# The running sum over the convolution's channels: in one row behind the last tap, not between the taps

## The chip, the cores and the metric

The kernel runs on one core of a Trainium2 chip. The metric is the device time of one execution in microseconds (us). The core's engines run side by side and meet only at semaphores: PE (TensorE, matrix products), DVE (VectorE), ACT (ScalarE), POOL (GpSimd) and SP (SyncE, which starts transfers).

## The reference, cut to what matters

Two layers of a decoder trunk over 528 tokens (16 meta tokens and 512 of the sequence), width 1024, in float32:

```
u = rms_norm(h, norm_mix); proj = u @ w_in          # glu, q, k, v, gates
a = glu_a * sigmoid(glu_b)
a = causal_depthwise_conv(a, conv_w, conv_b)        # 31 taps per channel
a = silu(layer_norm(a, conv_ln_g, conv_ln_b))       # mean and variance over the 1024 channels
y_conv = a @ w_pw + b_pw
y_attn = rms_norm(diff_attention(q, k, v, lam), subln)
h = h + (sigmoid(g_conv) * y_conv + sigmoid(g_attn) * y_attn) @ w_o
h = h + square(relu(rms_norm(h, norm_mlp) @ w_up)) @ w_down
```

The layer norm needs, for every token, the sum of the convolution's output over all channels. That sum is what the change moves.

## The kernel before, in words

Channels lie on the 128 partitions in eight tiles, tokens along the free dimension. Each layer runs as GLU (convolution inputs), five attention stages (0 to 4), a last part with the gates, the layer norm and the pointwise product, the output projection, and the MLP. Weights stream in as slabs of 128x2048, split into a high and a low half so that PE can multiply in three passes: POOL makes both halves (`split`, L505 to L518), and in the attention stages only the low half, in 16 pieces of 128x128 (`split_low`, L520 to L525), after ACT has made the high one. POOL also makes the rotary products of q and k (`turn`, L569 and L570).

The convolution is DVE's. The first 11 taps of six tiles are made in the GLU part, the remaining 182 (list `LATE`, two tiles at a time) in the attention stages by the generator `late_taps`. A tap is one instruction over 128x512 that accumulates in PSUM (L461, L462); the last tap of a tile writes it to `conv` in SBUF. DVE's order in the stages is written out by hand in `VECTOR_ORDER`: a number is so many taps, the names stand for the attention's steps (`m` maxima, `c` combination, `sub` mean square, `q`/`k` evictions, `rq`/`rk` rotation, `g` an early gate's eviction), and `ln`, in stage 4, stands for the rest of the taps and `ln_sums`. PE's order is in `MATRIX_ORDER`. Both engines work strictly in these orders.

The running sum is kept in `r_inv2[:, META:T]`. Behind the last tap of tile 1 tiles 0 and 1 are added (L473), behind those of tiles 3 and 5 two tiles each (L476), all inside `late_taps`; `ln_sums` adds tile 6 (L1397) and announces it with the semaphore `ln_ready`. PE sums that tile and tile 7 over the partitions with a product by ones (`channel_sums`, L674). Ahead of it stand these two waits on PE, of which the second is for the eviction of the last early gate:

```python
pe.wait_ge(exp_done, (layer + 1) * HEADS * 2 * 3)
pe.wait_ge(a_free[1], (layer * A_TILES + A_GATE + EARLY_GATES) // 2)
channel_sums(layer, ln_ready, layer + 1, [r_inv2[:], conv[:, NT - 1, :]], st_full)
```

On DVE that eviction (L1292, the `g` behind `ln`) follows `ln_sums`. PE's last work in stage 4, ahead of these waits, is the end of that gate, transposes, and the product with the values (`pv`, L745). When PE has used the gates' slab, POOL may split the next one into the same buffer (L514, L515, L517).

Of the kernel before, what the change touches and what calls it, by code (L numbers as in the profile page):

```python
# [26 lines left out]
ALU = mybir.AluOpType  # L27
# [10 lines left out]
NT = D // P  # L38
SEQ = 512
META = 16  # L40
T = META + SEQ
TAPS = 31
# [52 lines left out]
class Count:  # L95
# [12 lines left out]
    def link(self, ins, back=0):  # L108

        self.mark(ins)  # L110
        if self.off is not None or self.n > back:
            self.eng.wait_ge(self.sem, self.value(back))
# [9 lines left out]
def announce(eng, ins, sem, value):  # L122

    ins.then_inc(sem, 1)
    eng.wait_ge(sem, value)
# [16 lines left out]
def span(layer):  # L142


    return (0, T, 2) if layer < LAYERS - 1 else (META, SEQ, 1)
# [97 lines left out]
def build(nc, x_t, w_slabs, pvecs, rows_in, ident_in, mask_in, identb_in, out, h_spill, r_rows):  # L243
    ctx = ExitStack()
    with ctx:
# [8 lines left out]
        def at(name, shape, dt, offset):  # L254
            return nc.alloc_sbuf_tensor_at(name, shape, dt, offset=offset)
# [6 lines left out]
        conv = at("conv", [P, NT, T], F32, r_a)  # L262
# [51 lines left out]
        def small(name, shape, dt=F32):  # L314
            n = int(np.prod(shape[1:])) * (2 if dt == BF16 else 4)
            return at(name, shape, dt, region(n))
        r_inv = small("r_inv", [P, T])
        o_sq = small("o_sq", [P, T])
        r_inv2 = small("r_inv2", [P, T])
# [47 lines left out]
        ln_ready = sem("ln_ready")  # L367
# [83 lines left out]
        def conv_tap(layer, first, ch, k, begins, ends):  # L451

            w = pvec[:, ds(first * TAPS + (V_CW + ch * TAPS + k), 1)]
            x = xg[:, ds(first + ch, 1), META + k:k + T]
            done = conv[:, ds(first + ch, 1), META:T]
            bank = CONV_BANK[ch % 2]
            acc = psum[:, bank:bank + 1, 0:SEQ]
            if k == 0:  # L460
                return nc.vector.tensor_scalar(acc, x, w, pvec[:, ds(first + (V_CB + ch), 1)], ALU.mult, ALU.add)  # L461
            return nc.vector.scalar_tensor_tensor(out=done if ends else acc, in0=x, scalar=w, in1=done if begins else acc, op0=ALU.mult, op1=ALU.add)  # L462

        def late_taps(chain, layer):


            for ch, k in LATE:
                chain.link(conv_tap(layer, 0, ch, k, k == EARLY and ch < EARLY_TILES, k == TAPS - 1), back=1)
                if k == TAPS - 1 and ch % 2 and ch < NT - 1:
                    part = r_inv2[:, META:T]  # L470
                    chain.eng.wait_ge(chain.sem, chain.value())
                    if ch == 1:
                        chain.link(nc.vector.tensor_tensor(part, conv[:, 0, META:T], conv[:, 1, META:T], ALU.add))  # L473
                    else:
                        for x in (ch - 1, ch):
                            chain.link(nc.vector.tensor_tensor(part, part, conv[:, x, META:T], ALU.add))  # L476
                yield


# [642 lines left out]
        def _(dve):  # L1122
            chain = Count(dve, v_chain)
            link = chain.link
            V = nc.vector
# [173 lines left out]
            for layer in range(LAYERS):  # L1299
                lo, n, k = span(layer)  # L1300
# [82 lines left out]
                announce(dve, V.memset(raw[:, :, 0, :], 1.0), raw_clear, layer + 1)  # L1383

                taps = late_taps(chain, layer)

                def some_taps(m):
# [3 lines left out]
                def ln_sums():  # L1391

                    if layer < LAYERS - 1:
                        dve.wait_ge(conv_head, 1)
                        chain.mark(V.tensor_reduce(r_inv2[:, 0:META], conv[:, 0:NT - 1, 0:META].rearrange("p c m -> p m c"), AX_X, ALU.add))
                    dve.wait_ge(v_chain, chain.value())
                    announce(dve, V.tensor_tensor(r_inv2[:, META:T], r_inv2[:, META:T], conv[:, NT - 2, META:T], ALU.add), ln_ready, layer + 1)  # L1397

                for stage in range(5):
                    h0, gates = 2 * stage - 2, iter(range(EARLY_GATES))  # L1400
                    for name in VECTOR_ORDER[layer]["zero" if stage == 0 else "first" if stage == 1 else "last" if stage == 4 else "mid"].split():
                        what, arg = name.rstrip("012-"), name.lstrip("kmcsub")
                        if name.isdigit():
                            some_taps(int(name))
                        elif name == "stats":
                            rope_stats(layer, stage - 1)
                        elif name == "rk":
                            rope(layer, stage - 1, 1)
                        elif name == "rq":
                            rope(layer, stage, 0)  # L1410
                        elif name == "q":
                            qk_evict(layer, stage - 1, "q")
                        elif what == "k":
                            qk_evict(layer, stage - 1, "k", int(arg))
                        elif what == "m":
                            maxima(layer, h0 + int(arg[0]), int(arg[1]))
                        elif what == "c":
                            combine(layer, h0 + int(arg))
                        elif what == "sub":
                            mean_square(layer, h0 - 1 if arg == "-" else h0 + int(arg))  # L1420
                        elif name == "g":
                            gate(layer, next(gates))
                        elif name == "ln":
                            for _ in taps:
                                pass
                            ln_sums()
# [161 lines left out]
```

## Time and profile before

| | |
|---|---|
| median of 3 runs | 1889.38 us (1884.28 to 1890.79) |
| the profiled execution | 1887.12 us, its span in the trace 1885.3 us |
| PE busy | 1835.2 us, 97% of the span |
| DVE busy | 1221.5 us, 65% |
| POOL busy | 1114.6 us, 59% |
| ACT busy | 546.9 us, 29% |
| the late and early taps (L462) | 301.6 us, 440 instructions |

A share is an average over all stages. Idle time of an engine counts only where another one waits for it. Line numbers are those of the kernel before.

### The profile page before, as it was taken

What the parts mean: (1) busy time and instruction counts of PE and PEld (TensorE: products, weight loads), DVE (VectorE), ACT (ScalarE), POOL (GpSimd) and SP (SyncE); (2) the same over time, 40 slices, a digit from 0 to 9 for tenths busy, and PEclk for the clock granted to TensorE, in tenths of its full rate; (3) what the DMA queues carried; (4) which work ended last, traced back from release to release, by engine and by line L of the source; (5) the groups of instructions that cost most, each with busy time, mean ns of one, the idle gap of its engine ahead of it and who ended that gap; (6) DMA issues with size and microseconds to landing.
All of it is one profiled execution on the core that took longest, in us unless ns stands there. A gap on an engine that the chain in (4) does not pass through costs nothing. (4 is left out here: it accounts for less than half of the span.)

```text
span 1885.3 us, 33580 instructions
## 1 busy us (share of the span) xinstructions
PE 1835.2 (97%) x12743; PEld 1653.7 (88%) x12743; DVE 1221.5 (65%) x1665; ACT 546.9 (29%) x1598; POOL 1114.6 (59%) x1112
## 2 busy tenths in 40 slices
PE   7999999999999999999999999999999899999999
PEld 7999888889999999999999988877777678888887
DVE  6998988877654443333569978887787544434443
ACT  4135565435212201010111255644361122010100
POOL 3656455535766666666656564354357566777664
PEclk9999999999999999999999999999999999999999
DMA  4221011112322222223322221111133122222221
GB/s 175 89 90 68 24 68 46 46 68 92 139 88 88 89 90 89 92 90 110 113 104 90 77 81 37 55 46 51 62 112 135 67 93 99 98 89 89 94 107 67
DMA packets 25404, 160.63 MB, mean 85 GB/s; under 512 B 3009, under 2 KB 3393, under 8 KB 7505
## 3 DMA queue, kind: packets, MB, share of 16 engines
q1 hardware_dynamic: 21744, 147.01, 21.9%
q10 hardware_dynamic: 3552, 12.15, 1.8%
q8 instruction: 73, 1.20, 0.3%
q14 instruction: 35, 0.28, 0.0%
HBM read 154.85 MB, written 4.29 MB: 84 GB/s over the span
## 5 line engine op out<-in xcount | busy, mean ns | idle before, releaser
L626 PE MATMUL psum<-u,w_hi 128*128 128x264 f32 (+1 forms) x4480 | 915.6, 316 | 24.9 <-DMA identb<-identb 12.2
L626 PEld LDWEIGHTS psum<-u,w_hi 128*128 128x128 f32 x4480 | 679.7, 190 | 83.2 <-issue 18.8
L517 POOL TENSOR_TENSOR w_lo<-w_raw,w_hi 128x512 fp32r<-128x512 f32 x440 | 632.4, 1467 | 9.2
L626 PE MATMUL psum<-u,w_lo 128*128 128x264 f32 (+1 forms) x2240 | 567.2, 314 | 0.0
L626 PEld LDWEIGHTS psum<-u,w_lo 128*128 128x128 f32 x2240 | 369.4, 190 | 25.4
L686 PE MATMUL psum<-w_hi,u 128*128 128x256 f32 (+1 forms) x1856 | 339.2, 285 | 5.5 <-ACT v_sb L897 2.9
L514 POOL TENSOR_TENSOR tick<-ones 128x1 f32<-128x1 f32 x110 | 23.4, 213 | 501.7 <-PE psum L626 501.7
L462 DVE SCALAR_TENSOR_TENSOR psum<-xg,pvec,psum 128x512 f32<-128x512 f32 x440 | 301.6, 750 | 4.6 <-DVE xg L1347 2.2
L686 PEld LDWEIGHTS psum<-w_hi,u 128*128 128x128 f32 (+1 forms) x1856 | 265.1, 173 | 15.2 <-issue 4.6
L686 PE MATMUL psum<-w_lo,u 128*128 128x256 f32 (+1 forms) x928 | 260.5, 281 | 0.0
L524 POOL TENSOR_TENSOR w_lo<-w_raw,w_hi 128x128 fp32r<-128x128 f32 x384 | 188.4, 530 | 75.7 <-DVE raw L1194 30.8
L515 POOL TENSOR_SCALAR w_hi<-w_raw 128x2048 fp32r<-128x2048 f32 x110 | 211.5, 1922 | 0.0
L1489 DVE TENSOR_TENSOR relu<-relu 128x528 f32<-128x528 f32 (+1 forms) x64 | 78.2, 1222 | 202.6 <-ACT u L1104 104.7
L1102 ACT ACTIVATE relu<-psum 128x528 f32<-128x528 f32 (+1 forms) x64 | 38.8, 606 | 461.9 <-PE psum L626 461.9
L626 PE MATMUL psum<-hid_b,w_hi 128*128 128x264 f32 (+1 forms) x768 | 163.6, 321 | 0.0
L686 PEld LDWEIGHTS psum<-w_lo,u 128*128 128x128 f32 (+1 forms) x928 | 159.9, 172 | 4.1
L1518 DVE TENSOR_TENSOR down_tmp<-psum,r_inv 128x512 f32<-128x512 f32 (+1 forms) x56 | 39.1, 699 | 171.2 <-PE psum L626 171.2
L626 PEld LDWEIGHTS psum<-hid_b,w_hi 128*128 128x128 f32 x768 | 118.7, 188 | 11.5
L569 POOL TENSOR_TENSOR rtmp<-raw,tabs 128x640 f32<-128x640 f32 x16 | 25.0, 1565 | 163.1 <-DVE q_scale L1180 111.2
L626 PE MATMUL psum<-hid_b,w_lo 128*128 128x264 f32 (+1 forms) x384 | 102.2, 320 | 0.0
L937 ACT ACTIVATE e<-psum,nb,q_scale 128x272 f32<-128x272 f32 (+4 forms) x144 | 84.0, 586 | 44.1 <-DVE nb L1224 44.0
L1519 DVE TENSOR_TENSOR h<-h,down_tmp 128x512 f32 (+1 forms) x56 | 88.0, 1572 | 9.1 <-DVE down_tmp L1518 9.1
(184 smaller groups left out, 1969.9 us busy)
## 6 DMA issues: line engine op xcount, KB each, us to landing
w_raw<-w_slabs SPq DMA_DIRECT2D x136, 1024.0 KB, 4.8
h<-x_t SPq DMA_DIRECT2D x4, 528.0 KB, 7.5
h<-x_t ACTq DMA_DIRECT2D x1, 2112.0 KB, 8.2
h_spill<-h ACTq DMA_DIRECT2D x8, 264.0 KB, 2.0
h<-h_spill ACTq DMA_DIRECT2D x1, 2112.0 KB, 9.3
out<-h SPq DMA_DIRECT2D x8, 256.0 KB, 2.0
r_b<-r_rows ACTq DMA_DIRECT2D x1, 1584.0 KB, 7.2
r_b<-r_rows ACTq DMA_DIRECT2D x1, 1536.0 KB, 10.1
```

The source lines that it names most:

```text
L462: return nc.vector.scalar_tensor_tensor(out=done if ends else acc, in0=x, scalar=w, in1=done if begins else acc, op0=ALU.mult, op1=ALU.add)
L515: chain.link(nc.gpsimd.tensor_scalar(w_hi[:, b, :], w_raw[:, b, :], 1.0, 1.0, ALU.mult, ALU.mult))
L517: last = nc.gpsimd.tensor_tensor(w_lo[:, b, c:c + SLAB // 4], w_raw[:, b, c:c + SLAB // 4], w_hi[:, b, c:c + SLAB // 4], ALU.subtract)
L524: last = nc.gpsimd.tensor_tensor(w_lo[:, b, c:c + P], w_raw[:, b, c:c + P], w_hi[:, b, c:c + P], ALU.subtract)
L569: nc.gpsimd.tensor_tensor(t4[:, :, :, 0:H2], x4[:, :, :, H2:HD], mid4(tabs[:, x, 1, :, 0:H2], 4), ALU.mult)
L626: last = nc.tensor.matmul(psum[:, 2 * slot + j, 0:n], w[:, b, cut], src[:, part, kc, at0:at0 + n], start=(kc == 0 and m == 0), stop=(kc == ...
L686: last = nc.tensor.matmul(psum[0:tn, n % 2, 0:2 * P], u[:, part, kc, t0:t0 + tn], w[:, b, kc * 2 * P:(kc + 1) * 2 * P], start=(kc == 0 and ...
L937: ins = nc.scalar.activation(e[0:tn, c, E_OFF[i]:E_OFF[i] + w], psum[0:tn, banks[c], S_AT[i]:S_AT[i] + w], ACT.Exp, bias=nb[0:tn, c, i:i + ...
L1102: nc.scalar.activation(row(relu[:, j, :], layer), a_ps(layer, j), ACT.Relu).then_inc(a_free[j], 1)
L1489: link(V.tensor_tensor(relu2[:, lo:lo + n], relu[:, j, lo:lo + n], relu[:, j, lo:lo + n], ALU.mult))
L1518: announce(dve, V.tensor_tensor(row(down_tmp[:], layer), a_ps(layer, j), row(r_inv2[:], layer), ALU.mult), a_free[j], a_read(layer, A_MLP ...
L1519: ins = V.tensor_tensor(rown(h, ch, layer), rown(h, ch, layer), row(down_tmp[:], layer), ALU.add)
```

## The change

The generator of the late taps no longer adds anything. `ln_sums`, which runs after the last tap, makes the whole running sum: tile 0 plus tile 1, then tiles 2 to 6 one after the other, each waiting for the one before, and the last announces `ln_ready`. The number of additions (six per layer), their operands and their shape stay the same.

```diff
             for ch, k in LATE:
                 chain.link(conv_tap(layer, 0, ch, k, k == EARLY and ch < EARLY_TILES, k == TAPS - 1), back=1)
-                if k == TAPS - 1 and ch % 2 and ch < NT - 1:
-                    part = r_inv2[:, META:T]
-                    chain.eng.wait_ge(chain.sem, chain.value())
-                    if ch == 1:
-                        chain.link(nc.vector.tensor_tensor(part, conv[:, 0, META:T], conv[:, 1, META:T], ALU.add))
-                    else:
-                        for x in (ch - 1, ch):
-                            chain.link(nc.vector.tensor_tensor(part, part, conv[:, x, META:T], ALU.add))
                 yield
...
                     dve.wait_ge(v_chain, chain.value())
-                    announce(dve, V.tensor_tensor(r_inv2[:, META:T], r_inv2[:, META:T], conv[:, NT - 2, META:T], ALU.add), ln_ready, layer + 1)
+                    for ch in range(1, NT - 1):
+                        ins = V.tensor_tensor(r_inv2[:, META:T], conv[:, 0, META:T] if ch == 1 else r_inv2[:, META:T], conv[:, ch, META:T], ALU.add)
+                        if ch < NT - 2:
+                            link(ins)
+                        else:
+                            announce(dve, ins, ln_ready, layer + 1)
```

## Rows read from the trace of the kernel before

**Rows 1.** Attention, layer 1: stretch, length, PE busy (instructions), clock, DMA share, GB/s.
```profile
1060.00:1369.00 309.00, 294.49 (x2164) 0.98 0.16 55
```

**Rows 2.** Who waited for whom, PE: total, times, longest; layer 1, then layer 0.
```profile
PE psum L713 <- DVE o_ms L1252: 6.6, 2, 3.6
PE psum L686 <- POOL w_lo L524: 1.6, 1, 1.6
...
PE psum L626 <- DVE sg L1292: 1.2, 1, 1.2
...
PE psum L686 <- POOL w_lo L524: 1.0, 1, 1.0
```

**Rows 3.** Each layer's first addition: ns min/median/max, first and last start.
```profile
L473 DVE TENSOR_TENSOR r_inv<-conv x2: 692/692/692, 158.5 to 1113.2; 128x512 f32<-128x512 f32 x2
```

**Rows 4.** In order of time (start, us, instruction): DVE, layer 1, stage 2.
```profile
1177.98 1.42 DVE L476 TENSOR_TENSOR r_inv<-r_inv,conv 128x512 f32<-128x512 f32 x2
1184.50 1.23 DVE L1218 TENSOR_REDUCE mx<-psum 128x2 f32<-128x1024 f32 x1 [0.30 <-PE psum L721]
```

**Rows 5.** In order of time: layer 0, stage 1, then POOL's same product in layer 1.
```profile
160.72 1.49 DVE L1188 TENSOR_TENSOR raw<-raw,tabs 128x1280 f32<-128x1280 f32 x1 [0.24 <-POOL rtmp L570]
...
158.52 2.06 POOL L570 TENSOR_TENSOR rtmp<-raw,tabs 128x640 f32<-128x640 f32 x1
...
1102.74 1.56 POOL L570 TENSOR_TENSOR rtmp<-raw,tabs 128x640 f32<-128x640 f32 x1
```

**Rows 6.** POOL's line L524 from 1112.9 to 1114 us: ns min/median/max.
```profile
L524 POOL TENSOR_TENSOR w_lo<-w_raw,w_hi x2: 456/688/919, 1112.8 to 1113.2; 128x128 fp32r<-128x128 f32 x2
```

**Rows 7.** In order of time: PE and DVE, layer 1, stage 3.
```profile
1251.01 0.27 PE L721 MATMUL psum<-maskb,identb 128*128 128x112 bf16 x2
...
1257.69 0.28 PE L721 MATMUL psum<-maskb,identb 128*128 128x128 bf16 x2
1264.44 0.82 PE L713 MATMUL psum<-qk 64*128 64x272 f32 x4 [3.56 <-DVE o_ms L1252]
...
1252.09 1.22 DVE L1218 TENSOR_REDUCE mx<-psum 128x2 f32<-128x1024 f32 x1
...
1258.66 0.98 DVE L1218 TENSOR_REDUCE mx<-psum 128x2 f32<-128x800 f32 x1
```

**Rows 8.** In order of time: layer 0, end of stage 4; DVE, POOL, PE.
```profile
420.26 0.69 DVE L1397 TENSOR_TENSOR r_inv<-r_inv,conv 128x512 f32<-128x512 f32 x1
423.60 0.71 DVE L1292 TENSOR_TENSOR sg<-psum,r_inv 128x528 f32<-128x528 f32 x1 [2.65 <-PE psum L626]
...
423.79 1.90 POOL L515 TENSOR_SCALAR w_hi<-w_raw 128x2048 fp32r<-128x2048 f32 x1
...
426.75 1.16 PE L674 MATMUL psum<-r_inv,ones 128*128 128x264 f32 x4
```

**Rows 9.** In order of time: layer 1, end of stage 4; DVE, POOL, PE.
```profile
1360.93 0.69 DVE L1397 TENSOR_TENSOR r_inv<-r_inv,conv 128x512 f32<-128x512 f32 x1
...
1364.24 1.90 POOL L515 TENSOR_SCALAR w_hi<-w_raw 128x2048 fp32r<-128x2048 f32 x1
...
1367.08 1.12 PE L674 MATMUL psum<-r_inv,ones 128*128 128x512 f32 x2
```

**Rows 10.** In order of time: POOL and DVE, layer 0, behind the variance.
```profile
449.46 1.92 POOL L515 TENSOR_SCALAR w_hi<-w_raw 128x2048 fp32r<-128x2048 f32 x1
...
449.48 2.46 DVE L1155 SCALAR_TENSOR_TENSOR ln_rs<-ln_t,ln_rs 128x528 f32<-128x528 f32 x1
```

**Rows 11.** PE's busy time and clock by stretch; then the chain that ended last.
```profile
1350.00:1351.00 1.00, 1.00 (x4) 0.50 0.73 156
...
1346.49 0.70 DVE sg L1292
...
1347.33 4.58 PE psum L626 x12
1352.87 2.87 PE psum L626 x12
```

## The prediction

> **What bounds the kernel now.** The profiled execution took 1887.12 us, its span and 1.8 us around it. I read first PE's busy time by stage: in layer 1's attention stages, up to the point where PE sums the channels, it is 294.5 of 309 us [rows 1]. So these stages are PE's, and an edit on DVE can shorten them only where PE stands still for DVE, or for something that DVE holds up. The second view, who waited for whom, gives these places: two waits on the mean-square eviction (6.6 us together) and one on the low half of a weight slab (1.6 us) in layer 1, one on the same low half (1.0 us) in layer 0 [rows 2]. PE's other waits there hang on exponentials, value evictions or transposes whose chains the additions touch only through the times already counted below. The third view, the instructions in order of time, was then read around each removed addition and around the row of additions that replaces them.
>
> **What is removed.** Five additions of 128x512 per layer: one behind channel tile 1, two behind tile 3, two behind tile 5. Undisturbed one is 0.69 us [rows 3]; a clean pair takes 1.42 us, so the pitch is 0.73 us [rows 4]. Ten instructions, 7.3 us of DVE's time at that pitch, leave the stages, and the waits for a tap's completion ahead of them with them. What each place gives PE:
>
> Layer 0, stage 1 (the addition at 158.5). Behind it DVE waits for POOL's rotary product until 160.72, so the 0.73 us would be lost in that wait. But the addition and POOL's second product overlap, and that product took 2.06 us, where the same one beside no addition took 1.56 us [rows 5]. Without the addition POOL ends 0.5 us earlier, the rotation behind it too, and with it the release of POOL's next low-half pass, for which PE waits 1.0 us. Gain 0.5 us; bounds 0 and the wait of 1.0 us.
>
> Layer 1, stage 1 (the addition at 1113.2). It lies inside POOL's pass of 16 pieces; around it one piece took 919 ns, the other 456 [rows 6]. PE waits 1.6 us for that pass [rows 2], so 0.46 us of it goes. Bounds 0 and 0.7 (the addition's own length).
>
> Layer 1, stage 2 (two additions at 1177.98). The maxima behind them start earlier by less than 1.45 us, but the next maxima, at 1184.50, already wait 0.30 us for PE [rows 4]: the chain starts anew there, and only DVE's wait grows. The PE wait that follows is the larger part of 3 us, and none of it goes. Gain 0; bounds 0 and 0.45 us.
>
> Layer 1, stage 3 (two additions, begun behind the first maxima). Here the second maxima start at 1252.09 with no wait ahead of them, while PE's mask had ended at 1251.01+0.27 = 1251.28: they can come 0.75 us earlier. From there DVE runs without a gap to the third maxima at 1258.66, whose scores end at 1257.69+0.28 = 1257.97, so 0.63 us of it survive. Exponentials, combination and mean square follow without another release from PE, and PE's scores at 1264.44, which waited 3.56 us, start 0.63 us earlier [rows 7]. Gain 0.63 us; bounds 0 and 1.46 us, a pair's two pitches.
>
> Layer 0, stages 2 and 3 (two pairs). PE has no wait in reach whose chain runs through them: 0.
>
> Sum of gains: 0.50+0.46+0+0.63 = 1.6 us. PE is the bound between these places, so each gain is carried on.
>
> **What is added.** `ln_sums` issues six additions instead of one, in a row, each behind the completion of the one before: five more at a pitch of 0.73 us, 3.65 us of DVE. No DMA moves, and no queue of SP or ACT is passed. Queued behind them on DVE is the eviction of the eighth early gate; for it wait PE, which may start the channel sums only when that bank is free, and POOL's split not at all. In front lies idle time: layer 0's addition ends at 420.95 and the gate starts at 423.60, after 2.65 us of waiting for PE. So the bare row ends 1.0 us past the gate's start; the gate would end near 425.3, and PE's sums start at 426.75, behind the product with the values. The 3.65 us are then hidden: 2.65 by DVE's wait, 1.0 by that product.
>
> But the sixth addition meets POOL. The end of PE's gate work that releases the gate also releases POOL's split of the next slab: its pass over the high halves starts at 423.79 and lasts 1.90 us, and the sixth addition is due at 420.26+5x0.73 = 423.91 [rows 8]. What such a meeting costs stands at 449.46: DVE's instruction, two operands in SBUF, began 0.02 us behind POOL's pass and took 2.46 us [rows 10]. So in layer 0 the sixth addition ends at 426.37, the gate at 427.12, and with 0.15 us to PE's start (as from the gate's end at 1347.19 to PE's 1347.33, rounded up [rows 11]) the sums begin at 427.27 instead of 426.75: 0.52 us late. In layer 1 the first addition starts at 1360.93, the sixth is due at 1364.58, behind POOL's pass at 1364.24, which the fifth addition holds back till about 1364.55 [rows 9]. It ends at 1367.03, the gate at 1367.76, PE starts at 1367.91 instead of 1367.08: 0.83 us late. Cost 1.35 us; bounds 0 (the addition gets in first, and the gate's cover stands) and 2.6 us (blocked once more as long in one of the layers). PE's order behind the sums (gate tile, squares, variance) is a straight chain, so the delay is kept.
>
> The Trainium skill ("SBUF — State Buffer", section on the two sides of the memory) says that VectorE, with two SBUF inputs, and GpSimd take their shared port pair by an exclusive lock held for the whole instruction, whichever starts first. By that rule the cost is all or nothing: 1.35 us where POOL's pass starts first, none where the addition does. The trace agrees as far as the 2.46 us go.
>
> **Sum.** -1.6+1.35 = -0.25 us: 1886.9 us against the profiled execution. That one lies 2.3 us under the median of the three runs shown, 1889.38; against the median I forecast 1889.1. The three runs spread from 1884.28 to 1890.79, 6.5 us, so the change is far under what can be seen.
>
> **Rivals.**
> *A. No meeting at the end.* POOL's pass finds the sixth addition already started in both layers. In layer 0 the two are due 0.12 us apart, in layer 1, where POOL is held back by the fifth addition, about 0.03; either order can come out. Then the row is free and the gain stays: -1.6, 1887.8 us against the median. Against it: the meeting at 449.46 was as close and POOL won [rows 10]. The Trainium skill's rule of the exclusive lock, above, allows this outcome as well as mine.
>
> *B. The clock falls at the new wait (slower than before).* Ahead of 1347.33 PE stood 1.2 us for a gate's eviction on DVE [rows 2], behind the same product with the values; the granted clock then fell from 1.00 (2.4 GHz) to 0.50 (1.2 GHz), and twelve gate products took 4.58 us where they later took 2.87 [rows 11]. The waits of 0.5 and 0.8 us that I expect lie behind just such a product. If the clock falls after both, 2x1.7 = 3.4 us are added: -0.25+3.4 = +3.2, 1892.5 us. [...] Against it: the mean clock of the 309 us is 0.98 [rows 1], with longer waits than the new ones among them, so the clock doesn't fall far or often.
>
> *C. Nothing is gained earlier.* The earlier DVE and POOL work shifts other meetings of the two, which eat the 1.6 us, while the end costs 1.35: +1.35, 1890.7 us. For it: pieces of either engine double when they meet, and half of the gain is such a meeting avoided. Against it: DVE sits idle between most steps.
>
> *D. Passages at half speed shorten.* A mean clock of 0.98 over 309 us [rows 1] is about 12 us at the lower clock, some of it behind the waits that now shrink. With one such passage gone, 1.7 us more are gained: 1887.4 us.
>
> *E. The meaning of the change fails:* the compiled order might keep an addition in place or the waits behind it might stay. The diff leaves no such path; under 0.01.
>
> **How the numbers follow.** Forecast 0.5, A 0.15, B 0.12, C 0.13, D 0.1. The likeliest one's own range, by the bounds of its terms, is 1887 to 1890.5; the cases reach 1887 to 1892.5. The median of a few runs moves by some 2 us either way with a spread of 6.5 us, so the range is 1885 to 1893. A measurement of this kernel can tell from no change about 0.3%, 5.7 us. No case reaches that by its mechanism alone; only B with an unlucky set of runs, or A or D with a lucky one: faster 0.07, same 0.86, slower 0.07.
>
> **What would show it.** Right: no addition before the last tap of tile 7; POOL's second rotary product in layer 0, stage 1 near 1.55 us; PE's wait on the low half 0.5 us shorter in both layers; the 3.56 us wait near 2.9 and the one before it unchanged at 3.0; five additions of 0.69 us and a sixth of about 2.4 in each layer, and a new PE wait of 0.5 and 0.8 us ahead of the channel sums. Wrong: a sixth addition of 0.69 us (A), a granted clock of 0.50 behind the new waits (B), PE's waits in the stages unchanged in sum (C), or a median more than 5.7 us away, which none of these steps can explain.

## The result, and the profile after

The kernel after took 1876.14 us (median of 4 runs, 1874.49 to 1880.05), the kernel before on the same chip 1890.09 us (4 runs, 1884.28 to 1892.43): ratio 0.9934, 95% interval 0.9906 to 0.9961. That is some 12 us faster by the ratio, 14 by the medians; the forecast was 0.25 us, and 1876.14 lies 9 us under the range. The profiled executions differ by 11.0 us: 1876.08 us with a span of 1874.3, against 1887.12 with 1885.3. Of the runs below, one execution of row_long took 2148.79 us at a mean granted clock of 0.78, and its ratio leaves that one out.

The steps that were predicted are there. The page of the kernel after and its view of who waited for whom (us in total, times, longest):

```profile
span 1874.3 us, 33574 instructions
PE 1830.2 (98%) x12743; PEld 1650.8 (88%) x12743; DVE 1218.3 (65%) x1665; ACT 547.4 (29%) x1598; POOL 1112.2 (59%) x1112
```

```profile
PE psum L705 <- DVE o_ms L1244: 6.1, 2, 3.0
...
PE psum L618 <- DVE u L1464: 2.6, 2, 1.5
PE psum L678 <- POOL w_lo L516: 1.5, 2, 0.8
...
PE psum L666 <- DVE sg L1284: 0.6, 1, 0.6
```

The waits on the mean square fell from 6.6 to 6.1 us, those on the low half from 2.6 to 1.5 [rows 2], and a new one of 0.6 us stands ahead of the channel sums. But one line answers to none of my rows: PE's wait on `u`, the input of the output projection, is 2.6 us. Before it was 6.4 us, in three waits of up to 4.5:

```profile
PE psum L626 <- DVE u L1467: 6.4, 3, 4.5
```
The page also counts six instructions fewer, 33574 against 33580; the additions are as many as before, so these six are the waits that went with them.

Next, the places that answer to the rows ahead of the prediction, in order of time (start, us, instruction): POOL's product in layer 0, stage 1 [rows 5]; layer 1, stage 1, 2 and 3 [rows 2, 7]; the end of stage 4 in layer 0 and in layer 1 [rows 8, 9].

```profile
158.81 1.58 POOL L562 TENSOR_TENSOR rtmp<-raw,tabs 128x640 f32<-128x640 f32 x1
...
1115.07 0.50 PE L678 MATMUL psum<-w_hi,u 128*128 128x256 f32 x2 [0.72 <-POOL w_lo L516]
...
1195.28 1.21 PE L705 MATMUL psum<-qk 64*128 64x272 f32 x18 [3.04 <-DVE o_ms L1244]
...
1262.18 1.05 PE L705 MATMUL psum<-qk 64*128 64x272 f32 x6 [3.01 <-DVE o_ms L1244]
```

```profile
420.98 5.32 DVE L1390 TENSOR_TENSOR r_inv<-r_inv,conv 128x512 f32<-128x512 f32 x5
423.86 1.89 POOL L507 TENSOR_SCALAR w_hi<-w_raw 128x2048 fp32r<-128x2048 f32 x1
426.33 0.71 DVE L1284 TENSOR_TENSOR sg<-psum,r_inv 128x528 f32<-128x528 f32 x1
427.14 1.13 PE L666 MATMUL psum<-r_inv,ones 128*128 128x264 f32 x4 [0.32 <-issue]
...
1358.24 5.32 DVE L1390 TENSOR_TENSOR r_inv<-r_inv,conv 128x512 f32<-128x512 f32 x5
1361.12 1.89 POOL L507 TENSOR_SCALAR w_hi<-w_raw 128x2048 fp32r<-128x2048 f32 x1
1363.59 0.69 DVE L1284 TENSOR_TENSOR sg<-psum,r_inv 128x512 f32<-128x512 f32 x1
1364.38 1.10 PE L666 MATMUL psum<-r_inv,ones 128*128 128x512 f32 x2 [0.65 <-DVE sg L1284]
```

Five additions after the first take 5.32 us where five clean ones would take 5 x 0.73 = 3.65: the sixth met POOL's pass, in both layers, and the group's own statistics give its length:

```profile
L1390 DVE TENSOR_TENSOR r_inv<-r_inv,conv x5: 691/691/2415, 421.0 to 423.9; 128x512 f32<-128x512 f32 x5
```

So where are 11.0 us? I cut both spans at the same landmarks: PE's first channel sum of layer 1, the start of the first and the end of the last DVE instruction of the merge loop (the loop over eight channels that makes `u` from the pointwise product and the gates: L1459 to L1465 in the kernel after, L1462 to L1468 before), and a point behind. PE's busy time by stretch (length, PE busy, clock, DMA share, GB/s), first before, then after:

```profile
1060.00:1367.08 307.08, 292.57 (x2160) 0.98 0.16 56
1367.08:1429.10 62.02, 61.92 (x254) 1.00 0.30 105
1429.10:1479.43 50.33, 43.82 (x186) 0.99 0.37 135
1479.43:1506.00 26.57, 26.52 (x104) 0.90 0.16 56
```

```profile
1059.25:1364.38 305.13, 291.68 (x2159) 0.98 0.16 56
1364.38:1426.36 61.98, 61.87 (x253) 1.00 0.30 105
1426.36:1470.79 44.43, 43.01 (x186) 1.00 0.37 140
1470.79:1495.00 24.21, 24.15 (x104) 1.00 0.26 87
```

Everything up to layer 1's channel sums gives 2.70 us (1367.08 to 1364.38). The merge loop gives 5.90 (50.33 to 44.43) and the same 104 instructions of PE behind it 2.36 (26.57 to 24.21; granted clock 0.90 and 1.00). The sum is 10.96 of 11.0 us; what follows takes 379.30 us in both. Three quarters of the gain lie in and just behind a loop that the diff doesn't touch, over 60 us behind its last addition.

Both loops begin alike. DVE in the first turns, in order of time, before and then after (in brackets the idle time ahead and what ended it):

```profile
1433.21 0.69 DVE L1467 TENSOR_TENSOR u<-m_tmp,u 128x512 f32 x1 [0.98 <-ACT u L1084]
...
1436.50 1.67 DVE L1465 TENSOR_TENSOR m_tmp<-m_tmp,g_tmp 128x512 f32<-128x512 f32 x1
1439.52 1.60 DVE L1467 TENSOR_TENSOR u<-m_tmp,u 128x512 f32 x1 [1.35 <-ACT u L1084]
...
1445.32 2.37 DVE L1467 TENSOR_TENSOR u<-m_tmp,u 128x512 f32 x1 [0.98 <-ACT u L1084]
```

```profile
1430.48 0.69 DVE L1464 TENSOR_TENSOR u<-m_tmp,u 128x512 f32 x1 [0.99 <-ACT u L1076]
...
1433.77 1.67 DVE L1462 TENSOR_TENSOR m_tmp<-m_tmp,g_tmp 128x512 f32<-128x512 f32 x1
1436.43 0.71 DVE L1464 TENSOR_TENSOR u<-m_tmp,u 128x512 f32 x1 [1.00 <-ACT u L1076]
...
1441.79 0.69 DVE L1464 TENSOR_TENSOR u<-m_tmp,u 128x512 f32 x1 [0.98 <-ACT u L1076]
```

Shifted by 2.73 us the rows agree to 0.01, up to the second channel's subtraction to `u`. There DVE stands 1.35 us before and 1.00 after, although what it waits for comes at the same point in both: ACT's cast starts at 1438.32 and at 1435.58, 0.15 us behind the end of DVE's addition, and takes 0.62. DVE then starts 0.58 us behind the end of the cast before, and 0.23 us behind it after. Then POOL decides: before, a piece of its low-half pass had begun at 1439.3, and the subtraction took 1.60 us; after, the subtraction was first, took 0.71, and the piece was held up instead. From the next turn on the loops are different: at 1445.32 the subtraction falls into POOL's pass over the high half (1445.24, 1.91 us) and takes 2.37 us; after, it starts at 1441.79, ahead of that pass (1442.50), and takes 0.69. The two pieces of POOL by themselves, before and then after (ns min/median/max, first and last start); 1.74 us are those of a piece held up:

```profile
L517 POOL TENSOR_TENSOR w_lo<-w_raw,w_hi x1: 1287/1287/1287, 1439.3 to 1439.3; 128x512 fp32r<-128x512 f32 x1
```

```profile
L509 POOL TENSOR_TENSOR w_lo<-w_raw,w_hi x1: 1741/1741/1741, 1436.5 to 1436.5; 128x512 fp32r<-128x512 f32 x1
```

In every later turn the idle time before the second channel's subtraction is 1.10 to 1.12 us before, 0.99 after; before the first channel's it is 0.98 in both. Counting DVE's instructions in the compiled program from zero, the loop is instructions 1715 to 1742 before and 1709 to 1736 after, since three waits per layer are gone. (Waits, register instructions and branches count too; each stands once in the program, however often a loop passes it.) The second channel's subtraction is instruction 1740 before and 1734 after. This was the theory to test. It is called C in the experiments (the position of the code decides), with P (the place of the additions decides) and R (chance) against it. Later C was split in C1 (the stall belongs to a fixed number in the program) and C2 (it belongs to this instruction whenever the program is longer than some length), and M (the stall itself is small, the rest are meetings of DVE and POOL) was set against S (the stalls themselves cost the time).

### The profile page after: what moved, and what is told of

It is laid out like the page before. It is cut to its first block and busy times, and to the rows that moved or that the text cites. A ratio compares the mean times of both kernels' runs of the same rounds, so it can differ in the third digit from the quotient of the medians.

```text
span 1874.3 us, 33574 instructions
## 1 busy us (share of the span) xinstructions
PE 1830.2 (98%) x12743; PEld 1650.8 (88%) x12743; DVE 1218.3 (65%) x1665; ACT 547.4 (29%) x1598; POOL 1112.2 (59%) x1112
```

## The experiments

All ratios are to the kernel before, run beside them on the same chip. The runs were made on several chips, where the kernel before had medians of 1888.83 to 1890.09 us, so the ratios compare better than the medians. Each run's table row: median, ratio with interval, the position of layer 1's merge loop in DVE's program, its length in the profiled execution, and the longest PE wait on `u`.

| kernel | median us | ratio [95%] | loop at | loop us | wait us |
|---|---|---|---|---|---|
| before (again) | 1888.45 (one run) | | 1715 | 50.26 | 4.5 |
| after (again) | 1879.73 | 0.9955 [0.9941, 0.9969] | 1709 | 44.49 | 1.5 |
| row_long | 1890.27 | 1.0008 [0.9996, 1.0019] | 1715 | 50.28 | 4.5 |
| between_short | 1878.83 | 0.9950 [0.9933, 0.9966] | 1709 | 44.48 | 1.5 |
| pad3 | 1876.64 | 0.9948 [0.9931, 0.9965] | 1712 | 44.45 | 1.5 |
| pad19 | 1875.30 | 0.9931 [0.9914, 0.9949] | 1728 | 44.75 | 1.8 |
| pad134 | 1886.06 | 0.9985 [0.9976, 0.9995] | 1843 | 50.38 | 4.5 |
| before_small_low | 1863.48 | 0.9866 [0.9848, 0.9884] | 1715 | 44.20 | 0.4 |
| after_small_low | 1863.67 | 0.9861 [0.9840, 0.9881] | 1709 | 44.08 | 0.3 |
| delay_second | 1885.53 | 0.9982 [0.9972, 0.9992] | 1709 | 49.44 | 5.6 |
| delay_first | 1883.70 | 0.9975 [0.9963, 0.9987] | 1709 | 47.73 | 4.7 |
| delay_second_short | 1877.99 | 0.9946 [0.9930, 0.9963] | 1709 | 44.68 | 1.7 |
| delay_first_short | 1877.24 | 0.9942 [0.9925, 0.9958] | 1709 | 44.66 | 1.7 |
| layer0_pad29 | 1877.71 | 0.9949 [0.9931, 0.9967] | 1738 | 44.15 | 1.5 |
| layer0_pad93 | 1877.65 | 0.9943 [0.9924, 0.9963] | 1802 | 44.50 | 1.5 |
| gate_product_first | 1883.18 | 0.9967 [0.9955, 0.9978] | 1707 | 46.52 | 4.3 |

The 46.52 us of the last row run, like the others, from the first instruction that reads PE's tile; the product that this kernel makes ahead of it starts 1.59 us earlier.

### Place of the additions against position of the code

**row_long**: the kernel after, additions in one row, with six waits on DVE that have long been met when they are reached, one for each that the change removed.

```diff
                 chain.link(conv_tap(layer, 0, ch, k, k == EARLY and ch < EARLY_TILES, k == TAPS - 1), back=1)
+                if k == TAPS - 1 and ch % 2 and ch < NT - 1:
+                    chain.eng.wait_ge(pv_landed, 16 * (layer + 1))
+                    if ch != 3 or layer:
+                        chain.eng.wait_ge(rows_landed, 16 * (layer + 1))
```

> The changed kernel, additions in one row behind the last tap, with one satisfied wait more at each of the six places where a wait went with the additions, so that DVE's program again has as many instructions ahead of layer 1's merge loop as before (the loop starts at DVE instruction 1715, not 1709). Theory C (position of the code): the 0.35 us stall at the loop's second eviction to u comes back, the loop takes about 50.4 us instead of 44.5, PE waits over 4 us behind it and the clock falls; some 8 us slower than the changed kernel, about 1884 to 1886 us. Theory P (place of the additions): the loop keeps its 44.5 us and the time stays near 1876.

**between_short**: the kernel before, additions between the taps, with its separate wait for a tile's last tap folded into that tap's own link, so that DVE's program is as short as after.

```diff
-                chain.link(conv_tap(layer, 0, ch, k, k == EARLY and ch < EARLY_TILES, k == TAPS - 1), back=1)
+                chain.link(conv_tap(layer, 0, ch, k, k == EARLY and ch < EARLY_TILES, k == TAPS - 1), back=0 if k == TAPS - 1 and ch % 2 and ch < NT - 1 else 1)
                 if k == TAPS - 1 and ch % 2 and ch < NT - 1:
                     part = r_inv2[:, META:T]
-                    chain.eng.wait_ge(chain.sem, chain.value())
```

> The kernel before, additions between the taps, but the wait for the last tap is folded into that tap's own link, so that DVE's program is six instructions shorter and layer 1's merge loop starts at instruction 1709 as in the changed kernel. Theory C: the loop takes about 44.5 us, the clock stays up behind it, and the time falls by some 8 us to about 1880 us. Theory P: 50.4 us, and the time stays at 1887 to 1890.

**before_again** and **after_again**: the two kernels unchanged, profiled beside them.

> The kernel before once more, for a second profile. If what it showed is fixed by the program (theories C and P), the merge loop of layer 1 takes 50.4 us again, with the stall at its second eviction to u. If it is chance (theory R), the loop's length differs from the first profile's by more than 1 us.

> The changed kernel once more. Theories C and P: the merge loop of layer 1 takes 44.5 us again, and the ratio to the kernel before is 0.993 to 0.994. Theory R: the loop's length differs by more than 1 us, and the ratio may be nearer to 1.

With the two kernels themselves these make a square. Additions in one row: 0.9934 or 0.9955 with the short program, 1.0008 with the long one. Additions between the taps: 0.9950 short, 1 long. The place of the additions moves nothing that the intervals can tell, whichever the length; the length of the program moves some 10 us in both places. Two numbers missed what I had expected: row_long is slower than 1884 to 1886 us, and after_again's ratio lies over 0.993 to 0.994. P is refuted, and R with it, since loop lengths and idle times repeat: row_long's DVE shows the same stall at the same instruction as before,

```profile
1440.36 1.61 DVE L1468 TENSOR_TENSOR u<-m_tmp,u 128x512 f32 x1 [1.35 <-ACT u L1080]
```

and between_short's view by lines of the loop (busy us, mean ns, idle before) is the short one's, 700 ns a subtraction:

```profile
L1466 DVE TENSOR_TENSOR u<-m_tmp,u 128x512 f32 x8 | 5.6, 700 | 7.9 <-ACT u L1083 7.9
```

### The stall follows the instruction's number

**pad3** and **pad19**: the kernel after, with 3 or 19 memsets of one column (some 0.02 us each) on DVE in layer 1, ahead of its wait for the channel sums.

```diff
+                if layer == 1:
+                    for x in range(19):
+                        V.memset(padt[:, x:x + 1], 0.0)
                 dve.wait_ge(st_full, layer * 4 + 2)
```

> The changed kernel with 3 tiny memsets at the same place: the loop covers instructions 1712 to 1739, so that 1740 lies just behind it. Theory C1: no stall in the loop, 44.5 us, about 1878 us. Theory C2, or a boundary wider than one instruction: the stall at the second u comes back in part, 50 us and 1886 us.

> The changed kernel with 19 tiny memsets on DVE in layer 1 ahead of its wait for the channel sums, where DVE stands idle for over 4 us, so that the merge loop starts at DVE instruction 1728. Theory C1 (the stall belongs to a fixed place in the program, at instruction 1740): in the kernel before that was the second channel's subtraction to u; now it is the first channel's. The idle time before u is 1.1 to 1.4 us at the odd channels (first of each pair) and 0.99 at the even ones; whether the loop then takes 44.5 or 50 us depends on the meetings with POOL. Theory C2 (the stall belongs to this instruction whenever the program is longer than some length): 1.35 and 1.12 us at the second of each pair as before, about 50.3 us and 1887 us.

With 3 the loop ends at 1739, one short of 1740: idle times 0.98 to 1.00 throughout, 44.45 us. With 19 the first channel's subtraction is instruction 1740, and the stall has moved to it:

```profile
1429.74 0.69 DVE L1468 TENSOR_TENSOR u<-m_tmp,u 128x512 f32 x1 [1.33 <-ACT u L1077]
...
1435.60 0.71 DVE L1468 TENSOR_TENSOR u<-m_tmp,u 128x512 f32 x1 [1.00 <-ACT u L1077]
```

The later turns show 1.09 to 1.10 us before the first channel's subtraction and 0.99 before the second's, the mirror image of the kernel before. No POOL piece was near (the last one of the low half ends before 1427.2 us, the pass over the high half begins at 1430.45, behind the subtraction), the subtraction kept its 0.69 us, and the loop took 44.75. So the stalls by themselves lengthen the loop by 0.3 us, about the first of them: S is refuted by this run, and C2 with it, since the second channel's subtraction isn't late. The kernel before loses 6 us in the loop by where they fall.

**pad134**: 93 such memsets in layer 0 and 41 in layer 1.

```diff
+                for x in range((93, 41)[layer]):
+                    V.memset(padt[:, x:x + 1], 0.0)
                 dve.wait_ge(st_full, layer * 4 + 2)
```

> The kernel after with one-column memsets on DVE ahead of the wait for the channel sums: 93 in layer 0, 41 in layer 1 (0.02 us apiece). Layer 1's merge loop starts at instruction 1843 instead of 1709, so that its second channel's subtraction to u is instruction 1868 = 1740 + 128, the place that it had in the kernel before, one period of 128 later. If the place of the stall repeats every 128 instructions in layer 1: idle time before that u 1.35 us in the first turn, the loop takes 50 us, the PE wait behind it is 4.5 us, and the time is 1887 to 1891 us although nothing else differs from the kernel after. If it does not repeat (as nothing was seen in layer 0 at 844 and 908): idle time 0.98 to 1.00, loop 44.5 us, 1875 to 1879 us.

The stall is back, and with it the long loop and the wait:

```profile
1436.40 1.60 DVE L1467 TENSOR_TENSOR u<-m_tmp,u 128x512 f32 x1 [1.35 <-ACT u L1077]
...
1442.22 2.38 DVE L1467 TENSOR_TENSOR u<-m_tmp,u 128x512 f32 x1 [0.98 <-ACT u L1077]
```

```profile
PE psum L619 <- DVE u L1467: 6.4, 3, 4.5
```

134 tiny instructions gave back most of what six fewer had brought; the median, 1886.06, is just under the 1887 that I had expected. It is not the number 1740 alone, but 1740 and 1868, with nothing at 1734, 1737, 1753 or 1827, where the same subtraction stood in the other runs.

**layer0_pad29** and **layer0_pad93**: the same memsets in layer 0 alone.

```diff
+                if layer == 0:
+                    for x in range(29):
+                        V.memset(padt[:, x:x + 1], 0.0)
```

> The kernel after, with 29 memsets of one column each (0.02 us apiece, 0.5 us together) on DVE in layer 0, ahead of its wait for the channel sums. Layer 0's merge loop moves from instruction 790 to 819, so that its second channel's subtraction to u is instruction 844, which is 7 x 128 before 1740; layer 1's loop moves to 1738, where 1740 is its third instruction. If the place of the stall repeats every 128 instructions (or every 64 or 32): idle time before that u is about 1.35 us in the first turn and 1.12 in the later ones instead of 0.98, in layer 0's loop. If it does not repeat so: 0.98 throughout. By theory M a stall there may or may not throw layer 0's loop out of step (46.8 us in the kernel after), since POOL's pieces stand otherwise there; 46.8 to 50 us. Time 1876 to 1884 us.

> The same with 93 memsets, 64 more: the second channel's subtraction to u in layer 0 is instruction 908, and layer 1's loop starts at 1802, clear of 1740. If the period is 64 or 32, the idle times in layer 0's loop are those of the kernel with 29; if it is 128, they are 0.98 throughout (or the stall stands at another instruction) and the loop takes 46.8 us. Time 1875 to 1884 us. Layer 1's loop 44.5 us unless one of its instructions takes the stall at the second channel.

Neither shows a stall in layer 0's loop: 0.98 or 0.99 us before all eight subtractions, 46.79 and 46.78 us (after: 46.77). The first puts the second channel's subtraction at 844, which is 1740 less 7 x 128. So what holds at 1740 and at 1868 in layer 1 doesn't hold at 844 in layer 0.

layer0_pad29 shows the stall at 1740 a third time, in layer 1: there 1740 is the third instruction of the merge loop, just ahead of the loop's first work, and DVE stands 1.56 us in front of that work, against 1.20 in the kernel after.

```profile
1428.36 0.75 DVE L1463 SCALAR_TENSOR_TENSOR m_tmp<-psum,pvec,sg 128x512 f32<-128x512 f32 x1 [1.56 <-ACT sg L1046]
```

No subtraction is late by it, and the loop keeps in step.

The queue of instruction transfers (q14 in the page) goes along with the stall, but doesn't explain it. It moves one packet at 1440.2 in the kernel before, within the loop, and none within the loop of the kernel after, where it comes at 1473. In pad134 such a packet stands at 1437.1, within the loop again. But these packets start behind the stalled subtractions, which had started at 1439.52 and 1436.40; in pad19 the packet comes 3.4 us behind (1433.1 and 1429.74). So it isn't this packet that DVE waited for. And in layer0_pad29 one moved from 546.8 to 497.7, into layer 0's loop, and no stall is to be seen there.

### What turns 0.35 us into 8

**before_small_low** and **after_small_low**: both kernels with POOL's low halves outside the attention stages made for 16 of each 512 columns (the rest of the low half isn't computed). POOL then holds nothing for long in the merge loop but its pass over the high half.

```diff
-                    last = nc.gpsimd.tensor_tensor(w_lo[:, b, c:c + SLAB // 4], w_raw[:, b, c:c + SLAB // 4], w_hi[:, b, c:c + SLAB // 4], ALU.subtract)
+                    last = nc.gpsimd.tensor_tensor(w_lo[:, b, c:c + 16], w_raw[:, b, c:c + 16], w_hi[:, b, c:c + 16], ALU.subtract)
```

> The kernel before, with POOL's low halves outside the attention stages cut to 16 columns a piece instead of 512 (the rest of the low half isn't computed), so that POOL holds up DVE far less. Theory M (the stall itself costs under 1 us and the rest is lost by DVE and POOL meeting in another order): the merge loop of layer 1 takes under 44 us, with the 0.35 us stall still there, and this kernel and the changed one with the same cut differ by under 2 us. Theory S (the stalls alone make the difference): they still differ by 8 to 10 us.

> The changed kernel with the same cut (POOL's low halves outside the attention stages 16 columns a piece; the rest isn't computed). Theory M: within 2 us of the kernel before with that cut. Theory S: 8 to 10 us faster than it.

The difference between the two kernels is gone: 1863.48 and 1863.67 us, with ratios known to 0.2% either way. The stall isn't; this is the changed kernel before, in the loop's first turn:

```profile
1424.31 0.69 DVE L1467 TENSOR_TENSOR u<-m_tmp,u 128x512 f32 x1 [1.35 <-ACT u L1084]
```

With 1.35 us of idle time and then 1.11 to 1.12 its loop takes 44.20 us (44.08 in the other; I had expected under 44), PE then waits 0.4 us for `u`, and the granted clock is 1.00 in the 27 us behind. The 10 us thus need POOL's long pieces. Both kernels are also some 12 us faster than the kernel after: that is what the work on the low halves costs where it meets DVE, or is late for PE (the two weren't separated).

**delay_second** and **delay_first**: the kernel after with two small reductions, ahead of the subtraction of the second or of the first channel. The loop stays clear of 1740.

```diff
                         dve.wait_ge(m_hi, ch + (layer * NT + 1))
+                        if layer == 1 and j == 1:
+                            for x in range(2):
+                                V.tensor_reduce(padt[:, x:x + 1], ident[:], AX_X, ALU.max)
```

> The kernel after, with two small reductions over a constant (128x128 to 128x1, some 0.15 to 0.2 us each, one input) on DVE in layer 1's merge loop, behind the wait for the high half and ahead of the subtraction to u of every second channel. Their output is used nowhere. The loop starts at instruction 1709 and ends at 1738, so it stays clear of instruction 1740. Theory M (the stall at 1740 costs only its own few tenths, and the 6 us of the loop come from DVE and POOL falling out of step once the second channel's subtraction to u starts more than about 0.15 us later): the delay alone does it, the loop takes 49 to 51 us, the following PE wait on u is 3 to 4.5 us, and the time is 1884 to 1890 us. Theory C1 (only an instruction at that position loses the time, by something of its own that a delay does not copy): the loop takes 44.5 to 46 us (four times 0.35 us at most on top), 1876 to 1879 us.

> The same two reductions, but ahead of the subtraction to u of every first channel. Theory M (the meeting behind the second channel's subtraction is the sensitive one; a stall of 1.33 us instead of 0.98 before the first channel's did no harm): the loop takes 44.4 to 46 us and the time is 1875 to 1880 us, clearly under the kernel with the delay at the second channel. Rival (any delay of 0.3 us in the loop is enough): 49 to 51 us as there, 1884 to 1890 us.

The delay alone does it, which refutes what these two expectations call C1 (that the loss of time, and not only the stall, belongs to an instruction at that number). At the second channel, in the first turn:

```profile
1443.07 0.48 DVE L1467 TENSOR_REDUCE padt<-ident 128x1 f32<-128x128 f32 x2 [0.87 <-ACT u L1077]
1443.47 1.69 DVE L1468 TENSOR_TENSOR u<-m_tmp,u 128x512 f32 x1
```

The subtraction starts 1.27 us behind the end of the addition (1442.20) instead of 1.00, so the effective delay is 0.27 us, and it takes 1.69 us instead of 0.71; the loop takes 49.44 us. (This profiled execution, 1890.61 us, was the longest of its ten; the median is 1885.53.) The control was only half what I expected: at the first channel two turns kept in step, the third's subtraction took 2.35 us, and the loop 47.73; 1883.7 us, not 1875 to 1880. The second channel is then not the only sensitive place: a delay in every turn finds a meeting at either.

**delay_second_short** and **delay_first_short**: one reduction instead of two.

> The kernel after with one reduction (128x128 to 128x1, about 0.25 us) in layer 1's merge loop ahead of the subtraction to u of every second channel; its output is used nowhere. The loop is instructions 1709 to 1737. In the kernel after DVE could start that subtraction about 0.14 us ahead of POOL's pass. Theory M: 0.25 us put POOL's pass first in the first turn, u takes 1.6 to 1.7 us instead of 0.71, the loop 48 to 50 us, the PE wait on u 3 to 6 us, and the time is 1883 to 1889 us. Rival T (only a longer delay, or only its sum over the turns, does it): loop 44.5 to 45.5 us, 1876 to 1879 us.

> The same single reduction ahead of the subtraction to u of every first channel. With two of them (0.48 us) there the first two turns kept in step and the third lost it: loop 47.7 us. Theory M: with half of the delay the phases hold in all four turns: loop 44.4 to 45.2 us, 1875 to 1879 us. Rival (any repeated delay adds up over the turns): one of the later turns falls out of step, loop 46 to 48 us, 1880 to 1885 us.

Both kept in step. By my numbers delay_second_short should not have; its rows say why:

```profile
1437.28 0.29 DVE L1466 TENSOR_REDUCE padt<-ident 128x1 f32<-128x128 f32 x1 [0.87 <-ACT u L1077]
1437.48 0.68 DVE L1467 TENSOR_TENSOR u<-m_tmp,u 128x512 f32 x1
```

The reduction starts earlier than the subtraction would have (0.87 us of idle time, not 1.00) and overlaps it, so that the subtraction starts at 1437.48, 1.07 us behind the addition's end (1436.41): an effective delay of 0.07 us. Half of the dose that I had written down was never given. Between 0.07 us, harmless, and 0.27 us, which costs 5 us in the loop, lie the 0.14 us that I had estimated from the start of POOL's piece; the runs don't bring it closer. Since both short delays were harmless, they don't tell the two channels apart.

### A shorter chain in the loop

**gate_product_first**: the product of gate and attention output is made ahead of DVE's wait for PE.

```diff
+                        link(V.tensor_tensor(g_tmp[:, j:j + 1, lo:lo + n], sg[:, ds(ch * 2 + 1, 1), lo:lo + n], o_t[:, ds(ch, 1), lo:lo + n], ALU.mult))
                         a_wait(dve, layer, S_PW, A_PW, i, j)
...
-                        link(V.tensor_tensor(g_tmp[:, j:j + 1, lo:lo + n], sg[:, ds(ch * 2 + 1, 1), lo:lo + n], o_t[:, ds(ch, 1), lo:lo + n], ALU.mult))
```

> The kernel after, and in both layers' merge loops the product of the gate and the attention output (g_tmp, which needs nothing of PE's pointwise product) is made ahead of DVE's wait for PE instead of behind the addition that frees PE's bank. DVE's chain from PE's tile to u gets shorter by one instruction of 0.7 to 1.5 us per channel; that instruction then lies in DVE's wait for PE. Theory M (what costs is how DVE's and POOL's instructions meet): the chain is shorter but g_tmp moves into another part of POOL's pass, so that the loop takes 42 to 45 us if the shorter chain wins and up to 50 us if the phases get worse; the PE wait on u behind the loop (1.5 us in the kernel after) goes to 0 to 1 us in the first case. Time 1873 to 1877 us by the first, 1880 to 1888 us by the second.

The worse case came: 1883.18 us, 5 to 6 us over the two short delays, which ran beside it and keep the kernel after's time. The chain per channel is shorter, but the product, an addition or the subtraction now meets POOL's passes:

```profile
1442.71 0.69 DVE L1464 TENSOR_TENSOR u<-m_tmp,u 128x512 f32 x1 [0.98 <-ACT u L1076]
1443.70 2.38 DVE L1458 TENSOR_TENSOR g_tmp<-sg,o_t 128x512 f32 x1 [0.30 <-DVE u L1464]
...
1455.24 1.98 DVE L1464 TENSOR_TENSOR u<-m_tmp,u 128x512 f32 x1 [0.98 <-ACT u L1076]
```

PE then waits 4.3 us for `u`. It is the same mechanism from another cause: no stall, other phases. No version that computes everything beat the kernel after (pad19's 1875.30 is within its interval).

## Why the prediction was wrong

**What it got right.** *Layer 1, stage 3*: wait 3.01 us, 0.55 less (0.63 forecast). *Layer 1, stage 2*: 3.04, unchanged, as forecast. *Layer 1, stage 1*: the wait on the low half is 0.72 instead of 1.63, 0.9 less where I took 0.46. *Layer 0, stage 1*: POOL's second product takes 1.58 us, the wait falls by 0.2 instead of 0.5. *The row*: six additions in each layer, the sixth of 2.4 us behind POOL's pass, the sums 0.39 us late in layer 0 (0.52) and behind a wait of 0.65 in layer 1 (0.83). The gains come to some 1.65 us against 1.6, but by two errors that cancel, in the two stages 1. Rival A fell with that, and B and C too: the clock didn't fall behind the new waits, and the old ones did shrink. Of the sum, -0.25 us, the square says what can be said: 1.0008 against 1 with the long program, 0.9950 against 0.9934 and 0.9955 with the short one.

The profiled pair gives 2.70 us up to layer 1's sums, more than these terms, and two parts of it were in no term. One is 1.0 us in layer 0's output projection, where PE waited 0.82 us at 585.38 before and not at all after. Of all eighteen profiles that wait stands in three, before, before_again and row_long, and not in between_short: so the place of the additions doesn't make it. Ahead of it DVE's addition to `sumsq` took 1.75 us, and 0.71 after. The other is 1.5 us of rival D. Ahead of layer 1's last early gate PE stood 1.17 us before and 1.16 after, the granted clock then fell to 0.50 before and stayed at 1.00 after, and from the gate's first product to the scores behind it it took 4.51 and 2.98 us. But that isn't the change's doing, for in after_again the clock fell there again. By stretch, before, after and after_again:

```profile
1347.00:1353.00 6.00, 5.67 (x22) 0.72 0.44 158
...
1345.00:1351.00 6.00, 5.56 (x28) 1.00 0.44 154
...
1347.00:1353.00 6.00, 6.00 (x24) 0.72 0.49 179
```


**The step that failed** is the last half sentence on the removed parts: "and the waits for a tap's completion ahead of them with them". I took these waits for nothing but their time. They are six instructions, and with six fewer the later code of DVE stands at other numbers; that was a term of the sum, and I had put it at nothing without a reason. None of my rows lies behind the channel sums of layer 1. There the kernel before had a loop in which a stall of 0.35 us, at instruction 1740, put one subtraction behind a POOL piece instead of ahead of it. That cost 5.9 us in the loop, which PE saw chiefly as the wait of 4.5 us at its end. During that wait the granted clock fell to 0.50 (1.2 GHz), and it stayed there for 5.4 us behind it, another 2.4. The two together, 8.3 us, are what the runs showed in place of the forecast's nothing. The row of PE behind that wait shows it, 1.22 us for what takes 0.73 in the kernel after:

```profile
1479.48 1.22 PE L626 MATMUL psum<-u,w_hi 128*128 128x512 f32 x2 [4.48 <-DVE u L1467]
```

The second step that failed is the bound on chance: "No case reaches that by its mechanism alone" held only for the cases listed. The profile before did show the wait of 4.5 us on `u`, in the line that is third in the list of PE's waits, and a loop in which DVE's subtraction took 1.02 us on average where its shape takes 0.69. That was the largest thing that a shift of phases could move, either way, and a chance for it belonged in the list. That the change came out faster and not slower was luck: the number 1740 happened to leave the loop. The section on the chip says that the engines meet only at semaphores; DVE and POOL also hold each other up with no semaphore between them (a subtraction of 0.69 us alone took 1.60 behind a piece of POOL), and this loop hangs on it.

**Shown and not shown.** Shown: the position of the code decides and not the place of the additions (the square); the stall goes with the number in layer 1 (pad19, layer0_pad29, pad134); alone it costs 0.3 us (pad19, before_small_low); a delay without it makes the same loss (delay_second); without POOL's long pieces nothing of the difference is left. Not shown: what the stall is. q14's packet suggests that it has to do with bringing in instructions, but the packet comes behind the stall, and layer 0 speaks against it. Nor is it shown what makes the wait in layer 0's output projection.

## What to carry to other kernels

An edit that changes an engine's instruction count can move time far behind it, so compare a changed kernel also with one padded to the old length before crediting the edit. Look for loops in which two engines contend and meet within a few tenths of a microsecond: there a few tenths decide microseconds. Here the contention itself was worth some 12 us, as much again as the luck with its phase. And when a gain is larger than every term of its sum, cut both spans at the same landmarks first; four cuts found this one.

## What the runs showed of the hardware

**A stall tied to the place in the program.** In a loop, DVE stood some 0.35 us longer the first time that it reached instruction 1740 (or 1868) of its program, and 0.09 to 0.13 us longer at it in each later turn, with nothing else in the trace to end the wait. That was so with three different places of the loop at 1740 (before, pad19, layer0_pad29; in the last, 0.24 or 0.25 us in the later turns). At neither 844 nor 908 in layer 0.

**Meetings decide by who starts first.** The same subtraction took 0.69 us alone, 1.60 behind a low-half piece (1.29 us, begun 0.2 us earlier), and 2.37 behind the pass over a high half; where DVE was first it took 0.71 and POOL's piece 1.74. The Trainium skill ("SBUF — State Buffer", section "SBUF: two separate sides") has this as an exclusive lock for the whole instruction, the loser fully blocked; the trace agrees: 0.2 us of lateness cost 0.9 us at once, and the next meeting 1.7.

**Nearly the same work, 12 us apart.** Without POOL's long low-half pieces every addition and every subtraction of layer 1's merge loop took 0.69 us, and both kernels ended near 1863.5 us.
